# Matrix products with the operand pairs inside the thirds, a convolution slot cut into three pieces around the sample softmax, and a padded table of constants

## What is computed

```python
xn = rmsnorm(x, p["norm_mix_g"])
aq, ak, av, dq, dk, dvv, dz, da, db, ga, gb = split_cols(xn @ p["w_in"], IN_SPLITS)
...
ya = swa_prompt(aq, ak, av, p["sinks"])          # sliding window; swa_sample for the samples
qkv, new_dn_buf = causal_dwconv(jnp.concatenate([dq, dk, dvv], axis=-1), dn_buf, p["dn_conv_w"])
...
o, new_S = gated_delta(qh, kh, heads(dvv), g, beta, dn_state, chunk)
...
mix = jax.nn.sigmoid(ga) * (ya @ p["w_br_a"]) + jax.nn.sigmoid(gb) * (yb @ p["w_br_b"])
h = x + mix @ p["w_mix_out"]
...                                               # cross-attention to a memory, then
u, gv = jnp.split(rmsnorm(h, p["norm_ffn_g"]) @ p["w_up"], 2, axis=-1)
u, new_ffn_buf = causal_dwconv(u, ffn_buf, p["ffn_conv_w"])
h = h + (jax.nn.silu(u) * gv) @ p["w_down"]
```

## Time and profile before

| | |
|---|---|
| median of 3 runs | 1991.64 us (1991.51 to 1994.1) |
| the profiled execution: its own time / its span | 1987.64 us / 1985.8 us |
| PE busy | 1875.2 us (94%), 13,273 matmuls |
| PE weight loads busy | 1767.8 us (89%) |
| DVE / ACT / POOL busy | 957.8 / 489.5 / 831.7 us |
| granted TensorE clock, mean | 0.993 |
| HBM traffic over the span | 60 GB/s |

### The profile page before, as it was taken

One profiled execution on the slowest core, in us unless ns is written; L12 is line 12 of the kernel. 1 busy time (PEld: TensorE's weight loads), 2 busy tenths in 40 slices (PEclk: granted clock), 3 DMA queues, 4 the chain that ended last, 5 costly groups with the idle time before them and its releaser, 6 DMA issues.

```text
span 1985.8 us, 32389 instructions
## 1 busy us (share of the span) xinstructions
PE 1875.2 (94%) x13273; PEld 1767.8 (89%) x13273; DVE 957.8 (48%) x1150; ACT 489.5 (25%) x908; POOL 831.7 (42%) x907
## 2 busy tenths in 40 slices
PE   6988899999999899999999799999999999999997
PEld 6866799988887788998988699999999999999996
DVE  6877366764453231564141547344343444445346
ACT  6055326643222103412021533100010010000012
POOL 3411033331211223755664036555554555565465
PEclk9999999999999999999999999999999999999999
DMA  4311110110102121422222211111111111111112
GB/s 187 91 39 40 39 43 33 43 62 27 38 27 65 28 95 52 151 86 97 75 85 88 82 68 43 54 43 42 45 45 47 42 48 47 43 42 42 53 46 88
DMA packets 45483, 119.72 MB, mean 60 GB/s; under 512 B 3808, under 2 KB 20896, under 8 KB 44224
## 3 DMA queue, kind: packets, MB, share of 16 engines
q1 hardware_dynamic: 45392, 118.39, 17.9%
HBM read 102.94 MB, written 15.77 MB: 60 GB/s over the span
## 4 chain that ended last, share of the span: by engine, by line
PE 68%; DVE 7%; ACT 3%; issue 1%; POOL 0%; DVEq 0%; ACTq 0%; POOLq 0%
PE PS L544 42%; PE PS L1988 12%; PE PS L1378 3%; PE PS L1576 2%; PE PS L1870 1%; PE PS L1614 1%; PE PS L1770 1%; ACT TMP L1223 1%; DVE H L2651 1%; DVE XL L524 1%; PE PS L1935 1%; PE PS L2020 1%; PE PS L1661 0%; PE PS L1803 0%; DVE XL L2471 0%
## 5 line engine op out<-in xcount | busy, mean ns | idle before, releaser
L544 PE MATMUL PS<-XH,WH 128*128 128x352 f32 x2280 | 505.7, 330 | 34.2 <-POOL WL L759 14.0
L767 POOL TENSOR_TENSOR WH<-RAW,CST 128x256 fp32r<-128x256 f32 x288 | 195.2, 706 | 810.7 <-PE PS L544 409.3
L544 PE MATMUL PS<-XH,WL 128*128 128x352 f32 x2280 | 493.1, 324 | 0.0
L544 PE MATMUL PS<-XL,WH 128*128 128x352 f32 x2280 | 492.9, 324 | 0.0
L544 PEld LDWEIGHTS PS<-XH,WH 128*128 128x128 f32 x2280 | 389.3, 190 | 52.4 <-issue 34.9
L544 PEld LDWEIGHTS PS<-XH,WL 128*128 128x128 f32 x2280 | 392.8, 189 | 0.0
L544 PEld LDWEIGHTS PS<-XL,WH 128*128 128x128 f32 x2280 | 389.4, 189 | 0.0
L771 POOL TENSOR_TENSOR WL<-RAW,WH 128x256 fp32r<-128x256 f32 x288 | 260.6, 933 | 7.5
L2616 DVE TENSOR_TENSOR H<-H,PS 128x1056 f32<-128x1056 f32 x80 | 100.3, 1254 | 130.5 <-PE PS L1988 130.5
L757 POOL TENSOR_TENSOR WH<-RAW,CST 128x1024 fp32r<-128x1024 f32 x22 | 44.5, 2022 | 266.2 <-PE PS L544 139.7
L1285 ACT ACTIVATE AH<-TMP 128x1056 fp32r<-128x1056 f32 x20 | 20.8, 1081 | 359.0 <-PE PS L1988 345.5
(11 more groups left out here) (464 smaller groups left out, 2659.7 us busy)
## 6 DMA issues: line engine op xcount, KB each, us to landing
RAW<-in_w SPq DMA_DIRECT2D x136, 512.0 KB, 3.5
H<-in_xT SPq DMA_DIRECT2D x4, 1056.0 KB, 9.1
TMP<-in_xT SPq DMA_DIRECT2D x2, 2112.0 KB, 8.5
early_gates<-DV SPq DMA_DIRECT2D x18, 176.0 KB, 1.9
out_yT<-H SPq DMA_DIRECT2D x4, 704.0 KB
early_gates<-A SPq DMA_DIRECT2D x12, 176.0 KB, 1.8
DV<-early_gates SPq DMA_DIRECT2D x1, 2112.0 KB, 14.0
TMP<-early_gates SPq DMA_DIRECT2D x2, 1056.0 KB, 5.4
```

What stands on the lines that cost most here:

```text
L544: mm = nc.tensor.matmul(PS[:, 3 * mm_g + c, 0:CW], w_[:, p, off + k * P:off + (k + 1) * P], x_[:, xk0 + k, c * CW:(c + 1) * CW], start=fir ...
L767: nc.gpsimd.tensor_tensor(WH[:, p, c], RAW[:, p, c], one[:, 0:PIECE], ALU.mult)
```

## The change

Four edits. (1) In `gemm_part` and in `down` the third becomes the outer loop and the pair the inner one, and the pairs come as XH·WH, XH·WL, XL·WH (in the code's names WH·XH, WL·XH, WH·XL): nine matmuls on the same operands as before, in another order. (2) `dn` slot 0 is no longer a tile of its own behind the sample attention. It is cut by `k` into three pieces (27, 27 and 18 matmuls), put behind the gates' products, behind the transposes and behind the value products. (3) So that its banks 0 to 2 are free, the sample softmax's transposes go to banks 3 to 7; ACT copies the gates' third row (`gate_rows(2)`) ahead of them; and the value products alternate the two groups inside each `k`. (4) CST is padded from 502 to 512 float32 per partition.

```diff
-NCONST = _at
+NCONST = -(-_at // 64) * 64
...
-            for w_, x_ in ((WH, XH), (WH, XL), (WL, XH)):
-                for c in range(NCH):
+            for c in range(NCH):
+                for w_, x_ in ((WH, XH), (WL, XH), (WH, XL)):
                     first = k == 0 and w_ is WH and x_ is XH
-                    last = k == kn - 1 and w_ is WL
+                    last = k == kn - 1 and x_ is XL
...
             gate_rows(1)
+            gate_rows(2)
             for b in range(4):
                 act.wait_ge(ss_tp, b + 1)
                 nc.scalar.activation(s_pt[:, 2 * b:2 * b + 2, :, :],
-                                     PS[:, b, :].rearrange("p (k g n) -> p k g n", k=2, g=2),
+                                     PS[:, 3 + b, :].rearrange("p (k g n) -> p k g n", k=2, g=2),
...
-            gate_rows(2)
             act.wait_ge(ss_pv, 1)
...
+            def dn_first(a, b):
+
+                for k in range(a, b):
+                    mm = gemm_part(0, 0, k, KT)
+                    if k == KT - 1:
+                        mm.then_inc(w_used, 1)
+            pe.wait_ge(w_split, SLOTS["dn"][0] + 1)
+            pe.wait_ge(acc_free, acc0["dn"])
+            pe.wait_ge(ss_msk, 2)
+            dn_first(0, 3)
             pe.wait_ge(ss_p, 1)
+            pe.wait_ge(ab_row, 3)
...
+            dn_first(3, 6)
             pe.wait_ge(ss_pt, 5)
-            for g in range(2):
-                for k in range(NB):
-                    nc.tensor.matmul(PS[HD * g:HD * g + HD, 5, 0:CH], s_vc[:, k, HD * g:HD * g + HD], s_pt[:, k, g, :],
-                                     start=(k == 0), stop=False)
...
+            for k in range(NB + 1):
+                for g in range(2):
+                    v = s_vc[:, k, HD * g:HD * g + HD] if k < NB else s_v[0:TS, HD * g:HD * g + HD]
+                    pt = s_pt[:, k, g, :] if k < NB else s_pt[0:TS, NB, g, :]
+                    mm = nc.tensor.matmul(PS[HD * g:HD * g + HD, 7, 256:256 + CH], v, pt, start=(k == 0), stop=(k == NB))
             mm.then_inc(ss_pv, 1)
-
-
-            pe.wait_ge(ab_row, 3)
+            dn_first(6, KT)
...
-            pe.wait_ge(ss_y, 1)
-            pe.wait_ge(ss_pt, 5)
...
-            dn_tile(0, 0, False)
             dn_tile(1, 1, False)
...
-                        for w_, x_ in ((WH, AH), (WH, AL), (WL, AH)):
-                            for c in range(NCH):
+                        for c in range(NCH):
+                            for w_, x_ in ((WH, AH), (WL, AH), (WH, AL)):
```

More of the change, by code:

```diff
@@ L906, in _ @@
                 nc.scalar.activation(s_pt[:, 2 * b:2 * b + 2, :, :],
-                                     PS[:, b, :].rearrange("p (k g n) -> p k g n", k=2, g=2),
+                                     PS[:, 3 + b, :].rearrange("p (k g n) -> p k g n", k=2, g=2),
                                      ACT.Copy).then_inc(ss_pt, 1)
             act.wait_ge(ss_tp, 5)
-            nc.scalar.activation(s_pt[0:TS, 8, :, :], PS[0:TS, 4, 0:256].rearrange("p (g n) -> p g n", g=2),
+            nc.scalar.activation(s_pt[0:TS, 8, :, :], PS[0:TS, 7, 0:256].rearrange("p (g n) -> p g n", g=2),
                                  ACT.Copy).then_inc(ss_pt, 1)
-            gate_rows(2)
             act.wait_ge(ss_pv, 1)
-            nc.scalar.activation(YA[:, :, TP:T], PS[:, 5, 0:CH].rearrange("p (j n) -> p j n", j=NJ),
+            nc.scalar.activation(YA[:, :, TP:T], PS[:, 7, 256:256 + CH].rearrange("p (j n) -> p j n", j=NJ),
                                  ACT.Copy).then_inc(ss_y, 1)
@@ L1453, in _ @@
                     i = 2 * k + g
-                    mm = nc.tensor.transpose(PS[0:rows, i // 4, (i % 4) * CH:(i % 4) * CH + CH],
+                    mm = nc.tensor.transpose(PS[0:rows, 3 + i // 4, (i % 4) * CH:(i % 4) * CH + CH],
                                              s_s[:, g, k * CH:k * CH + rows], ident)
@@ L1457, in _ @@
                     mm.then_inc(ss_tp, 1)
+            dn_first(3, 6)
             pe.wait_ge(ss_pt, 5)
-            for g in range(2):
-                for k in range(NB):
-                    nc.tensor.matmul(PS[HD * g:HD * g + HD, 5, 0:CH], s_vc[:, k, HD * g:HD * g + HD], s_pt[:, k, g, :],
-                                     start=(k == 0), stop=False)
-                mm = nc.tensor.matmul(PS[HD * g:HD * g + HD, 5, 0:CH], s_v[0:TS, HD * g:HD * g + HD],
-                                      s_pt[0:TS, NB, g, :], start=False, stop=True)
+            for k in range(NB + 1):
[3 more added lines that the diff above has]
+                    mm = nc.tensor.matmul(PS[HD * g:HD * g + HD, 7, 256:256 + CH], v, pt, start=(k == 0), stop=(k == NB))
             mm.then_inc(ss_pv, 1)
-            pe.wait_ge(ab_row, 3)
+            dn_first(6, KT)
             for c in range(NBLK):
@@ L1990, in down @@
                                                       x_[:, k, bass.ts(c, CW)], start=(k == 0 and w_ is WH and x_ is AH),
-                                                      stop=(k == 1 and w_ is WL))
+                                                      stop=(k == 1 and x_ is AL))
                     mm.then_inc(w_used if m % 4 == 3 else f_down, 1)
@@ L2703, in layouts @@
              "w_ab": w_in[:, 2816:2824].reshape(KT, P, 8).transpose(1, 0, 2).reshape(P, 64)}
-    o["cst"] = A(np.concatenate([parts[k].astype(np.float32) for k in CONST], 1))
-    assert o["cst"].shape[1] == NCONST
+    o["cst"] = np.zeros((P, NCONST), np.float32)
+    for k, (a, n) in CONST.items():
+        o["cst"][:, a:a + n] = parts[k]
     pos = np.concatenate([np.arange(TP), np.tile(8192 + np.arange(LS), NB)]).astype(np.float32)
```

## The result

| | before | after |
|---|---|---|
| median | 1991.58 us (4 runs, 1989.93 to 1994.10) | 1965.65 us (4 runs, 1961.23 to 1968.49) |
| the profiled execution: time / span | 1987.64 / 1985.8 us | 1966.08 / 1964.3 us |

The ratio is 0.9867, with a 95% interval from 0.9845 to 0.9888: faster by 26 us, where 24.4 were forecast (1967 us).

What follows compares the result with a forecast made beforehand. PE, busy 94% of the span, was taken as the bound. Order 19.3 us plus slot 5.1 us made 24.4 us, so the profiled execution becomes 1963.2 us and the median 1967 us; range 1959 to 1988 us.

Steps and rivals of the forecast that it cites:

- Edit 1, the order: Large products: pace falls to 159.4 ns, saving 15.3 us in L544 and 4.0 us in L1988, 19.3 us together.
- A full DMA load therefore costs 2.1 ns a matmul: Two `out_chunk` runs, 161.2 ns with DMA engines full against 159.1 ns: the difference was put down to the transfers.
- The 0.3 ns drawn from it: Long stretches, DMA share 0.14: transfers add 0.3 ns to 159.1, giving the forecast pace of 159.4 ns.
- the price of the repeat: Large products, XH streamed twice in a row: at most 0.3 ns a matmul, 2.6 us either way, taken as nothing.
- 0.6 us, already in the 2.8 ns: Down product (L1988), streaming from AH and AL: alignment gives 0.4 ns a matmul, counted within its 2.8 ns gain.
- Edits 2 and 3, the slot: Sample softmax: 3.0 us of PE idle time covered, 2.25 us from alternated value products, less 0.2 us for restarts: 5.1 us.
- the cover: Before slot 2: ACT frees slot 0's banks at 251 us, PE asks at 258; 7 us must vanish before it costs.
- A faster PE meets no wall: POOL's splitting: it waits 4.01 us for PE before the next slot, and slots get only 0.2 us shorter.
- The order gives nothing: Rival, large products: something else sets 161.8 ns in long stretches, only 5.1 us remain, 1986.5 us; chance 0.15.
- Half of it: Rival, large products: part of the 2.7 ns is surroundings; 9.4 us plus 5.1, 1977 us; chance 0.15.
- The new order is slower: Rival, L544 and L1988: streaming XH twice while weights alternate brings SBUF's two readers into step; 2008 us; chance 0.12.
- The slot did not fail: Rival, sample softmax: a wait behind the moved softmax loses the slot's gain, 19.3 us remain, 1972 us; chance 0.03.

Runs made afterwards that it cites:

- 528: Changed kernel with CST padded to 528 float32 instead of 512: 1969.60 us, ratio 0.9903 to the kernel before; profiled again 1968.73 us, 0.9890.
- the two kernels above: Kernel before with only the third made the outer loop, unpadded: pairs in old sequence 1975.17 us (ratio 0.9932), in new sequence 1977.66 us (0.9937).
- the old pairs: Kernel before, unpadded, third outside, pairs kept as XH·WH, XL·WH, XH·WL: 1975.17 us, ratio 0.9932.
- 502: Changed kernel without the padding, CST at 502 float32 again: 1971.04 us, ratio 0.9909 to the kernel before.
- 504: Changed kernel with CST padded to 504 float32 instead of 512: 1971.18 us, ratio 0.9914 to the kernel before.

## Why the prediction was right

**Edit 1, the order** (19.3 us forecast). The reading of rows 4 and 5 against rows 2 was right: the pace is the order's and not that of short quiet runs. Over all starts of L544 less than 175 ns apart the mean went from 161.7 to 159.2 ns, 2.5 where 2.4 were forecast; the MLP is better than that (158.9), the levels of other stretches worse. These are 6,660 distances where the prediction had counted 6,370. The down product gained 3.3 ns for 2.8. That is 16.4 + 4.7 = 21.1 us at the counts of the traces.

Three things in it were luck. "A full DMA load therefore costs 2.1 ns a matmul" was wrong: rows 7 had caught another level of the same loop, and in the changed kernel the faster of the two `out_chunk`s is the one with the DMA engines full. The 0.3 ns drawn from it landed near the mean over all stretches for another reason. That the MLP's runs fell into the best level could not be known either: with 528 half of them stand at 161.1 ns, 0.7 below the old pace. And the price of the repeat was read from durations (rows 8), while a matmul's cost is the distance to the next start; that new and old pairs are the same was only shown by the two kernels above.

**Edit 4, the padding, is the step of the sum that failed.** "0.6 us, already in the 2.8 ns" took its worth from the old order and added it to the new as if the two were independent. They are not: without it the order costs the down product 0.9 ns (1.3 us) and with it it gains 3.3. The prediction's total came out, by luck, since it assumed the full pace for L1988 and the padding delivered it. Had the padding been absent, the forecast for edit 1 would have been 5.3 us too good (4.0 gained in it, 1.3 lost in the runs). The 0.5 us of the key and value products was not seen at all; that AH and AL are their operands stood in rows 8.

**Edits 2 and 3, the slot** (5.1 us). 5.35 measured, each part as worked out: both idle times gone, 2.2 us by the alternation, slot 1 at 245.98. What was mis-sized is the cover: 2.4 us of the 7 are eaten by DVE's wait for POOL, since POOL's split now falls where DVE's gate operations do and no longer beside the convolution.

**A faster PE meets no wall.** PE is at 94% as before, and POOL still waits for it for some 4 us a slot.

**The rivals.** "The order gives nothing" (1986.5) is excluded by the MLP's pieces, and with it a distance that no order moves. What spoke for it in rows 7 was a level. The Trainium skill, "TensorE: Matmul & The Clock Gate", section "Back-to-back issue gap", gives N/2.4 + 2.5 ns (an estimate of 149.2 ns for 352 columns) as the gap of isolated matmuls, and has weight load and matmul together set it in a stream, which the prediction had left out; the best pace here is 9.7 ns above that estimate. "Half of it" describes only stretches at the 160.0 ns level, as around 930 us. "The new order is slower" holds for the down product without padding, by 0.9 ns, but not by its mechanism: the old pairs, which never stream one operand twice in a row inside a third, lose as much there. The slot did not fail.

**The sum.** 16.4 + 4.7 + 0.5 + 5.35 = 27.0 us by the pieces, against 26 by the medians and 21.6 between the two profiled executions. Of the 5.4 us between the pieces and the executions 2.2 were given back in the cross-attention, where the granted clock was lower, and 1.4 in the delta rule; 1.8 I cannot place.

## What to carry to other kernels

When the same weights or columns are met several times in a tiled product, keep the streamed tile for several matmuls and change the operand pair inside: here this alone was 1.8% of the pace in the MLP. Check the byte address of every tile that PE reads against 128 before judging an order: the order that gained 2.9 ns on aligned operands lost 0.9 on a tile 40 bytes short. Do not read a cause from two short runs whose pace differs by 1 or 2 ns, for the same loop can stand at several levels. Two changes that touch the same operands are to be priced together, and a cheap alignment is worth trying again after each change of order.

## What was not expected of the hardware

- The start address matters on both sides of the array: counted from the start of CST, a streamed operand 40 or 32 bytes short of a multiple of 128 (502 and 504) has 163.1 ns for 352 columns where an aligned one has 158.9, in one order, and (40 bytes only) 162.2 against 161.9 in the other; weights 40, 32 or 64 bytes short make the 512-column matmul 233 ns and not 228.
- Long runs of one program stand at fixed levels 1.1 ns apart (158.9, 160.0, 161.1), repeated to 0.01 us for 288 matmuls, in places that a change elsewhere can shift. Each level is a sequence of distances of its own, from 155 to 162 ns or from 158 to 166, and `out_chunk` was at 159.1 or 161.2 whether the DMA engines were full or idle.
- Two DVE operations of 0.2 us stretched to 1.07 and 2.42 us beside a split on POOL, and so was one of the convolution before (2.38 us against 0.24).
